# The front by single k-tiles, squares in halves, four steps ahead, one row moved from pair 3 to pair 4

## The chip, the cores and the metric

One Trainium2 chip, one of its cores. The metric is the device time of one execution in microseconds, the median of several runs. The engines are PE (TensorE matmul; PEld is its weight load), DVE (VectorE), ACT (ScalarE), POOL (GpSimd) and SP (SyncE, which only issues DMAs here).

## What is computed

Two transformer blocks on 256 tokens of width 2048, all in float32. The first block, at whose beginning the change lies, is this (cut):

```python
mod = silu(c) @ w_ada + b_ada                       # c: (1, 2048), w_ada: (2048, 6144)
shift, scale, gate = jnp.split(mod, 3, axis=-1)
h = rms_norm(x, g) * (1.0 + scale[:, None]) + shift[:, None]
proj = jnp.einsum('bsd,df->bsf', h, w_in)           # 7168 columns
q_a, k_a, v_a, z_a, q_r, k_r, v_r, z_r = jnp.split(proj, IN_SPLIT_IDX, axis=-1)
# dilated attention, retention in both directions, gates, output projection, residual
```

The second block has differential attention, a shared K/V and forgetting attention, with three more modulation vectors of the same kind and projections of 2048 rows.

## The kernel before

**Weight steps.** All weights come in steps of 128 x 1024 float32 (512 KB), two k-tiles of 128 rows times a chunk of 512 columns. SP loads a step into raw (8 slots). ACT casts it to w_hi (4 slots, L1190, split_high), a rounded float whose product with another such PE takes in one pass. DVE takes the rest, raw - w_hi, into w_lo (L1652, split_low). PE adds three products for each tile: hi by w_hi (L814), hi by w_lo (L815), lo by w_hi (L816). That makes 12 matmuls in a step. The cast of step m waits until PE has ended step m - 4.

**The front.** Steps 0 to 79 (FRONT) are the projections q, k, v and the retention's parts, ten chunks of 512 columns (numbers 0 to 9) by 16 k-tiles. They begin before the whole activation is there: for k-tile kt, h needs entries kt of shift and scale, and each of these needs one row of w_ada (transposed, 1 MB) times silu(c). So there are 32 rows (numbers 0 to 31; rows 2kt and 2kt + 1 belong to k-tile kt). POOL loads a row into gw (3 slots, L683, function load) once the row three before has been used; DVE reduces it (L1660, gemv_step), and with the second row of a k-tile makes mod and scales (L1668, L1673, head_finish). ACT then makes hi and hi + lo of the k-tile (L1519, L1523, head_kt), and DVE takes lo (L1680, head_low). Chunks are summed in two parts (PARTED tells how many k-tiles the first has): the first part leaves its PSUM bank with ACT's keep_part (L1551), the second is added by DVE's add_part (L1715).

**Who does what when.** In front() ACT and DVE each go through the steps m = 2 to 83 in order, with hand-written tables of what comes behind the split of which step: ROW_AT (row g on DVE), LOW_AT (low part of k-tile kt on DVE) and SHIFT_AT (the k-tile on ACT). Rows 32 to 47, the gate's, lie in pairs 3 and 4; a pair is 16 steps, and the steps n = 64 to 79 are pair 4, where the attention of the first block runs too. PAIR_TILES gives the rows of a pair and gemv_steps their places. Row 48 and all behind it need silu of c_2, which POOL loads when row 47 has been used.

**Queues.** SP issues x's tile 1, the vectors, then the steps: step k waits until PE has used step k - 8, and for the first 24 (LEAD_STEPS) until split k - 6 (HEAD_LEAD) is done. Step 0 is issued once tile 1 of x has landed, step 2 once row 2 has. POOL issues rows 0 and 1 when the first half of tile 0 of x has landed, computes x's inverse root (L707, L717), and issues row 2 when step 0 has landed.

**The very start.** PE spreads c over the partitions (L777), ACT takes silu of it in four pieces (L1500) and squares tile 0 of x (L1506), DVE squares tile 1 (L1687), POOL makes the root, ACT and DVE scale one tile each (L1511, L1691), PE transposes (L787), ACT keeps the eight banks (L1535, head_keep).

Of the kernel before, what the change touches and what calls it, by code (L numbers as in the profile page):

```python
# [159 lines left out]
def gemv_steps(pair):  # L160

    n = PAIR_TILES.get(pair, 0)
    first = HEAD_TILES + sum(k for p, k in PAIR_TILES.items() if p < pair)


    if pair == 4:
        return [(h, first + i) for i, h in enumerate((0, 1, 3, 4, 6, 9, 10))]
    begin, end = {3: (0, 16), 5: (0, 15), 8: (1, 9), 18: (1, 9), 22: (0, 7), 9: (6, 16), 19: (5, 16)}.get(pair, (1, 14))
    return [(begin + i * ((end - begin) / n), first + i) for i in range(n)]
# [131 lines left out]
def two_blocks(nc, a, out):  # L301
# [34 lines left out]
    with ExitStack() as ctx:  # L336
# [81 lines left out]
        bias_first = sem("bias_first")  # L418
        x_begun = sem("x_begun")
        x_landed = [sem(f"x_landed{tt}") for tt in range(TT)]  # L420
# [45 lines left out]
        c_spread = sem("c_spread")  # L466
        xhat_ready = sem("xhat_ready")
        scales_ready = sem("scales_ready")
# [150 lines left out]
        def _(sp):  # L619


            sp.dma_start(c_row, a["c"]).then_inc(c_landed[0], 16)
            for n in range(2):
                cols = slice(n * D // 2, (n + 1) * D // 2)
                sp.dma_start(resid[:, 1, cols], a["x"][0, P:2 * P, cols]).then_inc(x_landed[1], 16)
            sp.dma_start(vecs[:], a["t_vecs"]).then_inc(vecs_landed, 16)
            sp.wait_ge(x_landed[1], 32)

# [41 lines left out]
        def _(pool):  # L670
# [24 lines left out]
            def inverse_root(key):  # L695
# [8 lines left out]
                elif key[0] == "x":  # L704
                    pool.wait_ge(consts_ready, 1)
                    pool.wait_ge(x_squared, TT)
                    nc.gpsimd.tensor_scalar(mean_sq[:], square_sums[:], 1.0 / D, NORM_EPS,  # L707
                                            ALU.mult, ALU.add).then_inc(x_meaned, 1)
                    pool.wait_ge(x_meaned, 1)
# [61 lines left out]
        def _(pe):  # L771
            def head():
# [6 lines left out]
                pe.wait_ge(ident_landed, 16)  # L779
                pe.wait_ge(xhat_ready, TT)  # L780
                for r in range(TURNS):
                    if r == 4:
                        pe.wait_ge(silu_ready, 1)
                    for tt in range(TT):
# [6 lines left out]
            def front_step(n):  # L791

                if n < 2:
                    pe.wait_ge(head_kept, 4 * (n + 1))
                for q, kt in FRONT[n]:
# [381 lines left out]
        def _(act):  # L1177

            for n, landed in enumerate((x_begun, x_landed[0])):
                cols = slice(n * D // 2, (n + 1) * D // 2)  # L1180
                act.dma_start(resid[:, 0, cols], a["x"][0, 0:P, cols]).then_inc(landed, 16)
            act.dma_start(ident[:], a["t_ident"]).then_inc(ident_landed, 16)
# [313 lines left out]
            def head_x():  # L1496

                def spread_silu(n):
                    act.wait_ge(c_spread, n + 1)
                    return nc.scalar.activation(c_act[:, n * CHUNK:(n + 1) * CHUNK], banks[4 + n][:], ACT.Silu)  # L1500

                spread_silu(0)
                spread_silu(1)
                act.wait_ge(x_begun, 16)
                act.wait_ge(x_landed[0], 16)
                nc.scalar.activation(area[:, Q, 0], resid[:, 0], ACT.Square,  # L1506
                                     accum_out=square_sums[:, 0:1]).then_inc(x_squared, 1)
                spread_silu(2)
                spread_silu(3).then_inc(silu_ready, 1)
                act.wait_ge(root_ready, 1)  # L1510
                nc.scalar.activation(area[:, Q, 0], resid[:, 0], ACT.Copy, scale=rstd[:, 0:1]).then_inc(xhat_ready, 1)  # L1511

# [110 lines left out]
        def _(dve):  # L1623
# [59 lines left out]
            def head():  # L1683

                nc.vector.memset(ones, 1.0).then_inc(ones_ready, 1)
                dve.wait_ge(x_landed[1], 32)
                nc.vector.tensor_tensor_reduce(out=area[:, Q, 1], in0=resid[:, 1], in1=resid[:, 1], scale=1.0,  # L1687
                                               scalar=0.0, op0=ALU.mult, op1=ALU.add,
                                               accum_out=square_sums[:, 1:2]).then_inc(x_squared, 1)
# [680 lines left out]
```

## Time and profile before

| | us |
|---|---|
| median of 3 runs (lowest, highest) | 1442.14 (1441.98, 1442.36) |
| the profiled execution's own time | 1439.39 |
| its span, first to last instruction | 1437.6 |
| first weight matmul (L814) begins | 21.91 |
| PE busy in the span | 1405.9 (98%) |

A page of the profile gives the busy time of each engine, the span in 40 slices, and groups of instructions by line. In the timeline a line is: start in us, duration in us, engine, line of the code, operation, what is written from what, and in brackets how long the engine had been idle and what released it. A matmul's duration there (0.39 us) is longer than its turn, since matmuls overlap: the distance between starts counts.

### The profile page before, as it was taken

Reading aid. Unit: us, or ns where it says so; the run is one execution under the profiler, and the core shown is the slowest. Engines: PE = TensorE matmul, PEld = TensorE weight load, DVE = VectorE, ACT = ScalarE, POOL = GpSimd, SP = SyncE. Lnnn points to the kernel's source line nnn. Section 1 sums busy time; section 2 is a strip of 40 time slices with the busy share of each in tenths; the row PEclk is TensorE's granted clock in tenths of the full one; section 3 lists DMA queues with packets and bytes.
Section 4 is the critical chain, followed back from the end, with each engine's and each line's share of the span. In section 5 each row is a group of like instructions: output and inputs, shape, how many; then the busy total and the mean of one; then the engine's idle time right before and its main releaser. Section 6 shows DMA issues by size and latency. Waiting matters only on the chain.

```text
span 1437.6 us, 19794 instructions
## 1 busy us (share of the span) xinstructions
PE 1405.9 (98%) x6934; PEld 1175.3 (82%) x6934; DVE 1190.0 (83%) x1533; ACT 708.1 (49%) x1039; POOL 141.2 (10%) x233
## 2 busy tenths in 40 slices
PE   6999999999999999999999999999999999999996
PEld 4778888888888788888888888878888888888885
DVE  6899899888998889898878789988797877667566
ACT  5554434755435644444455553464345545465441
POOL 1111011003100001110011100010010002110000
PEclk9999999999999999999999999999999999999999
DMA  9999999888996899999977799589799688775762
GB/s 356 412 411 415 413 403 384 314 310 301 413 415 214 297 346 382 403 377 367 350 227 253 241 347 407 192 295 357 255 348 341 211 312 273 230 251 174 266 192 98
DMA packets 101624, 450.97 MB, mean 314 GB/s; under 512 B 11729, under 2 KB 16161, under 8 KB 77857
## 3 DMA queue, kind: packets, MB, share of 16 engines
q1 hardware_dynamic: 68690, 247.63, 48.2%
q0 software_dynamic: 25584, 185.63, 33.4%
q10 hardware_dynamic: 7264, 16.55, 3.1%
q8 instruction: 55, 0.90, 0.3%
q14 instruction: 31, 0.25, 0.0%
HBM read 447.62 MB, written 2.15 MB: 313 GB/s over the span
## 4 chain that ended last, share of the span: by engine, by line
PE 87%; DVE 5%; DMA 3%; issue 2%; ACT 1%; POOL 0%; DVEq 0%; SPq 0%; ACTq 0%
PE bank L879 16%; PE bank L881 16%; PE bank L880 16%; PE bank L862 15%; PE bank L860 8%; PE bank L814 3%; PE bank L816 3%; PE bank L815 3%; PE bank L1109 2%; DVE gw L1660 2%; DMA raw<-in_t_steps 2%; PE bank L1067 2%; DVE w_lo L1652 2%; PE bank L858 1%; PE bank L827 1%
## 5 line engine op out<-in xcount | busy, mean ns | idle before, releaser
L1190 ACT CAST w_hi<-raw 128x1024 fp32r<-128x1024 f32 x436 | 457.6, 1051 | 611.0 <-PE bank L881 286.8
L1635 DVE TENSOR_TENSOR w_lo<-raw,w_hi 128x1024 fp32r<-128x1024 f32 x360 | 438.5, 1225 | 176.4 <-ACT w_hi L1190 174.9
L1660 DVE CUSTOM_DVE_ANT_0 gw<-gw,c_act 128x2048 f32<-128x2048 f32 x176 | 402.3, 2287 | 0.2 <-DMA gw<-in_t_mod 0.2
L880 PE MATMUL bank<-w_lo,act_parts 128*128 128x512 f32 x1024 | 398.8, 389 | 0.0
L879 PE MATMUL bank<-w_hi,act_parts 128*128 128x512 f32 x960 | 386.5, 403 | 0.6 <-issue 0.5
L881 PE MATMUL bank<-w_hi,act_parts 128*128 128x512 f32 x960 | 375.0, 391 | 0.0
L862 PE MATMUL bank<-act_parts,w_hi 128*128 128x512 f32 x960 | 338.4, 395 | 0.0
L860 PE MATMUL bank<-act_parts,w_lo 128*128 128x256 f32 x1024 | 276.9, 281 | 0.0
L880 PEld LDWEIGHTS bank<-w_lo,act_parts 128*128 128x128 f32 x1024 | 192.6, 188 | 38.0
L862 PEld LDWEIGHTS bank<-act_parts,w_hi 128*128 128x128 f32 x960 | 180.1, 188 | 39.2
L881 PEld LDWEIGHTS bank<-w_hi,act_parts 128*128 128x128 f32 x960 | 180.2, 188 | 38.9
L879 PEld LDWEIGHTS bank<-w_hi,act_parts 128*128 128x128 f32 x960 | 180.4, 188 | 37.7 <-issue 2.4
L860 PEld LDWEIGHTS bank<-act_parts,w_lo 128*128 128x128 f32 x1024 | 192.9, 188 | 5.5
L814 PE MATMUL bank<-w_hi,act_parts 128*128 128x512 f32 x320 | 127.6, 399 | 9.9 <-DVE act_parts L1680 6.1
L816 PE MATMUL bank<-w_hi,act_parts 128*128 128x512 f32 x320 | 125.2, 391 | 0.0
L815 PE MATMUL bank<-w_lo,act_parts 128*128 128x512 f32 x320 | 125.1, 391 | 0.0
L1652 DVE TENSOR_TENSOR w_lo<-raw,w_hi 128x1024 fp32r<-128x1024 f32 x84 | 101.2, 1222 | 11.9 <-ACT w_hi L1190 11.9
L683 POOL DMA_DIRECT2D gw<-in_t_mod x96 | 52.2, 544 | 548.5 <-DVE products L1660 534.3
L814 PEld LDWEIGHTS bank<-w_hi,act_parts 128*128 128x128 f32 x320 | 60.4, 189 | 26.3 <-issue 8.0
L816 PEld LDWEIGHTS bank<-w_hi,act_parts 128*128 128x128 f32 x320 | 60.4, 189 | 12.9
L815 PEld LDWEIGHTS bank<-w_lo,act_parts 128*128 128x128 f32 x320 | 60.5, 189 | 12.1
L683 POOL DMA_DIRECT2D gw<-in_t_ada x48 | 25.6, 533 | 198.4 <-DVE products L1660 190.5
(197 smaller groups left out, 1073.7 us busy)
## 6 DMA issues: line engine op xcount, KB each, us to landing
raw<-in_t_steps SPq DMA_DIRECT2D x464, 512.0 KB, 6.5
gw<-in_t_mod POOLq DMA_DIRECT2D x96, 1024.0 KB, 8.2
gw<-in_t_ada POOLq DMA_DIRECT2D x48, 1024.0 KB, 8.4
gw<-in_t_kv_mod POOLq DMA_DIRECT2D x32, 1024.0 KB, 8.2
area<-gate_rows ACTq DMA_DIRECT2D x3, 1024.0 KB, 13.3
bias<-forget_sums ACTq DMA_DIRECT2D x16, 192.0 KB, 6.4
area<-in_ln_g ACTq DMA_DIRECT2D x2, 1024.0 KB, 8.1
area<-in_ln_b ACTq DMA_DIRECT2D x2, 1024.0 KB, 12.2
```

The source lines that it names most:

```text
L814: nc.tensor.matmul(dst, hi, w_hi[:, n % LEAD, i], start=(kt == first), stop=False)
L815: nc.tensor.matmul(dst, hi, w_lo[:, n % SLOTS, i], start=False, stop=False)
L816: last = nc.tensor.matmul(dst, lo, w_hi[:, n % LEAD, i], start=False, stop=(kt == stop - 1))
L860: last = nc.tensor.matmul(bank[:, 0:SEQ], lo[:, cols], act_hi[:, kt], start=False, stop=False)
L862: last = nc.tensor.matmul(bank[:], hi[:, cols], act_parts[:, kt].rearrange("p b t -> p (b t)"), start=False, stop=(kt == KT - 1))
L879: nc.tensor.matmul(dst, hi, w[:, k], start=(kt == 0), stop=False)
L880: nc.tensor.matmul(dst, hi, w_lo[:, j % SLOTS, k], start=False, stop=False)
L881: return nc.tensor.matmul(dst, lo, w[:, k], start=False, stop=(kt == KT - 1))
L1190: nc.scalar.copy(w_hi[:, b], raw[:, j % SLOTS]).then_inc(hi_ready, 1)
L1635: nc.vector.tensor_tensor(w_lo[:, j % SLOTS], raw[:, j % SLOTS], w_hi[:, j % LEAD].bitcast(F32), ALU.subtract).then_inc(lo_ready, 1)
L1652: nc.vector.tensor_tensor(w_lo[:, j % SLOTS], raw[:, j % SLOTS], w_hi[:, j % LEAD].bitcast(F32), ALU.subtract).then_inc(lo_ready, 1)
L1660: nc.vector.tensor_tensor_reduce(out=w, in0=w, in1=c_act[:].rearrange("p (t n) -> p t n", t=TT), scale=1.0, scalar=0.0, op0=ALU.mult, op1= ...
```

## The change

Six things, all at the beginning. (1) FRONT's steps mostly hold one k-tile of two chunks and no longer two k-tiles of one chunk, where k-tiles are new; the same products are summed in the same banks. (2) x is squared in halves on both engines, into two columns that POOL adds; ACT scales tile 0 in halves, and the transposes start with the first. (3) HEAD_LEAD is 4, not 6; SP's step 0 waits for row 0 and no longer for x; POOL's rows 0 and 1 wait for the second piece of the spread c, row 2 for row 1, and row 4 for row 3 as well. (4) ROW_AT, LOW_AT and SHIFT_AT have new places. (5) ACT keeps two banks, casts step 0, keeps one, makes k-tile 0 and casts step 1, then keeps the rest; PE waits for as many kept banks as it overwrites; DVE waits for the vectors behind rows 0 and 1; add_part stands ahead of the split. (6) Pair 3 has 8 rows and not 9, pair 4 has 8 and not 7, with the last at half step 12.

```diff
-PAIR_TILES = {3: 9, 4: 7, 5: 10, ...
+PAIR_TILES = {3: 8, 4: 8, 5: 10, ...
-FRONT = [((0, 0), (1, 0)), ((2, 0), (4, 0)), ((2, 1), (4, 1)), ((0, 1), (1, 1))]
-FRONT += [((q, kt), (q, kt + 1)) for q, kt in
-          [(3, 0), (5, 0), (8, 0), (6, 0), (8, 2), (6, 2), (0, 2), (1, 2), (9, 0), (9, 2), (9, 4), (6, 4), (0, 4),
-           (1, 4), (7, 0), (7, 2), (7, 4), (0, 6), (1, 6), (6, 6), (7, 6)]
-          + [(q, kt) for q in (2, 4, 3, 5) for kt in (2, 4, 6)]
-          + [(q, kt) for kt in (8, 10, 12, 14) for q in (2, 4, 3, 5)]
-          + [(q, kt) for q in (0, 1, 8, 9, 6, 7) for kt in range(PARTED[q], KT, 2)]]
+FRONT = [((0, 0), (1, 0)), ((2, 0), (4, 0)), ((2, 1), (4, 1)), ((0, 1), (1, 1)), ((3, 0), (3, 1)), ((5, 0), (5, 1)),
+         ((8, 0), (8, 1)), ((6, 0), (6, 1))]
+FRONT += [((p, kt), (q, kt)) for kt in (2, 3) for p, q in ((8, 6), (0, 1))]
+FRONT += [((9, kt), (9, kt + 1)) for kt in (0, 2)]
+FRONT += [((p, kt), (q, kt)) for kt in (4, 5) for p, q in ((9, 6), (0, 1))]
+FRONT += [((7, kt), (7, kt + 1)) for kt in (0, 2, 4)]
+FRONT += [((p, kt), (q, kt)) for kt in (6, 7) for p, q in ((0, 1), (6, 7))]
+FRONT += [((q, kt), (q, kt + 1)) for q in (2, 4, 3, 5) for kt in (2, 4, 6)]
+FRONT += [((p, kt), (q, kt)) for kt in range(8, KT - 2) for p, q in ((2, 4), (3, 5))]
...
-HEAD_LEAD, LEAD_STEPS = 6, 24
-ROW_AT = {4: 4, 5: 5, 6: 6, 7: 7, 8: 9, 9: 10, 10: 12, 11: 13, 12: 15, 13: 16, 14: 18, 15: 20}
-ROW_AT.update({g: 22 + int((g - 16) * 1.65) for g in range(16, HEAD_TILES)})
-LOW_AT = {1: 2, 2: 6, 3: 8, 4: 12, 5: 14, 6: 18, 7: 21}
+HEAD_LEAD, LEAD_STEPS = 4, 24
+ROW_AT = {4: 4, 5: 5, 6: 6, 7: 8, 8: 10, 9: 12, 10: 14, 11: 15, 12: 17, 13: 19, 14: 21, 15: 22}
+ROW_AT.update({g: 24 + int((g - 16) * 1.65) for g in range(16, HEAD_TILES)})
+LOW_AT = {1: 2, 2: 6, 3: 9, 4: 13, 5: 16, 6: 21, 7: 23}
-SHIFT_AT = {1: 3}
-SHIFT_AT.update({kt: ROW_AT[2 * kt + 1] + (3 if kt < 8 else 2) for kt in range(2, KT)})
+SHIFT_AT = {1: 2, 2: 6, 3: 10, 4: 14, 5: 18, 6: 22, 7: 25}
+SHIFT_AT.update({kt: ROW_AT[2 * kt + 1] + 2 for kt in range(8, KT)})
...
-            sp.wait_ge(x_landed[1], 32)
...
+                if k == 0:
+                    sp.wait_ge(gw_landed[0], 16)
...
-                    pool.wait_ge(x_squared, TT)
-                    nc.gpsimd.tensor_scalar(mean_sq[:], square_sums[:], 1.0 / D, NORM_EPS,
+                    pool.wait_ge(x_squared, 2 * TT)
+                    nc.gpsimd.tensor_tensor(mean_sq[:], most_squares[:], square_sums[:], ALU.add
+                                            ).then_inc(x_meaned, 1)
+                    pool.wait_ge(x_meaned, 1)
+                    nc.gpsimd.tensor_scalar(mean_sq[:], mean_sq[:], 1.0 / D, NORM_EPS,
...
-            pool.wait_ge(x_begun, 16)
+            pool.wait_ge(c_spread, 2)
             load(0)
             load(1)
             inverse_root(("x",))
-            pool.wait_ge(raw_landed[0], 16)
+            pool.wait_ge(gw_landed[1], 16)
             for g in range(2, HEAD_TILES + GEMV_RING):
+                if g == 4:
+                    pool.wait_ge(gw_landed[0], 32)
                 load(g)
...
-            head_step(0)
-            for r in range(6):
+            for r in range(2):
+                head_keep(r)
+            head_step(0)
+            head_keep(2)
+            head_kt(0)
+            head_step(1)
+            for r in range(3, TURNS):
                 head_keep(r)
...
+                    if n >= 0:
+                        add_part(n)
                     split_low(m)
```

## Rows read from the trace of the kernel before

**Rows 1.** The page: busy us and share of the span of each engine.

```profile
PE 1405.9 (98%) x6934; PEld 1175.3 (82%) x6934; DVE 1190.0 (83%) x1533; ACT 708.1 (49%) x1039; POOL 141.2 (10%) x233
```

**Rows 2.** Windows: stretch, length, busy of PE, PEld, DVE, ACT, POOL; clock; DMA share; GB/s.

```profile
16.50:18.50 2.00, 2.00 (x13) 2.00 (x12) 2.00 (x3) 2.00 (x4) 1.13 (x2) 1.00 0.34 63
28.00:90.00 62.00, 54.93 (x230) 43.82 (x231) 55.35 (x68) 35.80 (x49) 6.86 (x13) 0.97 1.02 411
90.00:155.00 65.00, 64.85 (x285) 53.07 (x284) 64.52 (x74) 35.31 (x46) 7.39 (x14) 1.00 1.02 416
175.00:215.00 40.00, 39.32 (x175) 31.94 (x174) 40.00 (x43) 15.50 (x15) 4.22 (x8) 1.00 1.02 403
```

**Rows 3.** Timeline, 8 to 22 us, all engines.

```profile
9.65 2.29 DVE L1687 CUSTOM_DVE_ANT_0 area<-resid 128x2048 f32<-128x2048 f32 x1 [8.67 <-DMA resid<-in_x]
12.41 0.72 POOL L717 TENSOR_TENSOR rstd<-mean_sq,minus_half 128x2 f32<-128x2 f32 x1
14.37 2.28 DVE L1660 CUSTOM_DVE_ANT_0 gw<-gw,c_act 128x2048 f32<-128x2048 f32 x1
15.31 5.01 PE L787 MATMUL bank<-ident,area 128*128 128x128 f32 x32 [5.51 <-ACT area L1511]
16.29 1.05 ACT L1190 CAST w_hi<-raw 128x1024 fp32r<-128x1024 f32 x1 [1.12 <-DMA raw<-in_t_steps]
```

**Rows 4.** Timeline and windows (columns as in rows 2), 21 to 34 us.

```profile
21.91 0.47 PE L814 MATMUL bank<-w_hi,act_parts 128*128 128x512 f32 x1 [1.59 <-DVE act_parts L1680]
23.18 1.23 DVE L1652 TENSOR_TENSOR w_lo<-raw,w_hi 128x1024 fp32r<-128x1024 f32 x1 [1.42 <-ACT w_hi L1190]
28.10 1.04 ACT L1190 CAST w_hi<-raw 128x1024 fp32r<-128x1024 f32 x1 [4.95 <-DMA raw<-in_t_steps]
32.10 0.77 PE L814 MATMUL bank<-w_hi,act_parts 128*128 128x512 f32 x1 [4.49 <-DVE act_parts L1680]
...
28.00:30.00 2.00, 0.00 (x0) 0.00 (x0) 1.93 (x5) 1.66 (x2) 0.53 (x1) 1.00 1.01 412
32.00:34.00 2.00, 1.90 (x5) 1.54 (x6) 2.00 (x2) 1.19 (x2) 0.00 (x0) 0.50 1.02 422
```

**Rows 5.** Timeline, 45 to 85 us: k-tile 2, step 8, the cast of step 22.

```profile
45.10 0.43 DVE L1680 TENSOR_TENSOR act_parts<-side,act_parts 128x256 fp32r<-128x256 f32 x1 [3.79 <-ACT side L1523]
52.66 0.50 PE L814 MATMUL bank<-w_hi,act_parts 128*128 128x512 f32 x1 [0.67 <-DVE w_lo L1652]
84.53 1.05 ACT L1190 CAST w_hi<-raw 128x1024 fp32r<-128x1024 f32 x1 [1.67 <-PE bank L816]
```

**Rows 6.** DMA queues (q0 rows, q1 steps): 31 to 38, then 28 to 90 us.

```profile
q0 software_dynamic: 258, 1.97, 67.3%
q1 hardware_dynamic: 263, 0.95, 33.9%
raw<-in_t_steps SPq DMA_DIRECT2D x2, 512.0 KB, 12.3
...
q1 hardware_dynamic: 3250, 11.83, 47.3%
raw<-in_t_steps SPq DMA_DIRECT2D x21, 512.0 KB, 7.8
```

**Rows 7.** The same view, 18.5 to 25.5 us.

```profile
q1 hardware_dynamic: 12, 0.05, 1.8%
```

**Rows 8.** Chain that ended last, near 156 us, and the timeline near 200 us.

```profile
155.94 12.43 DMA raw<-in_t_steps
...
200.32 0.47 PE L814 MATMUL bank<-w_hi,act_parts 128*128 128x512 f32 x1 [0.68 <-DVE w_lo L1652]
```

**Rows 9.** Timeline of POOL and ACT, 249 to 263 us; landing of c_act.

```profile
249.85 0.53 POOL L680 DMA_DIRECT2D c_act<-in_c  x1 [3.08 <-DVE products L1660]
262.52 1.28 ACT L1494 ACT_TABLE_LOAD   x1
...
DMA to landing us min/median/max: 6.3/6.3/6.3
```

More of the change, by code:

```diff
@@ L114 @@
               {2: 0, 4: 1, 3: 3, 5: 2, 0: 0, 1: 1, 8: 0, 9: 1, 6: 0, 7: 1})
-FRONT = [((0, 0), (1, 0)), ((2, 0), (4, 0)), ((2, 1), (4, 1)), ((0, 1), (1, 1))]
-FRONT += [((q, kt), (q, kt + 1)) for q, kt in
-          [(3, 0), (5, 0), (8, 0), (6, 0), (8, 2), (6, 2), (0, 2), (1, 2), (9, 0), (9, 2), (9, 4), (6, 4), (0, 4),
-           (1, 4), (7, 0), (7, 2), (7, 4), (0, 6), (1, 6), (6, 6), (7, 6)]
-          + [(q, kt) for q in (2, 4, 3, 5) for kt in (2, 4, 6)]
-          + [(q, kt) for kt in (8, 10, 12, 14) for q in (2, 4, 3, 5)]
-          + [(q, kt) for q in (0, 1, 8, 9, 6, 7) for kt in range(PARTED[q], KT, 2)]]
+FRONT = [((0, 0), (1, 0)), ((2, 0), (4, 0)), ((2, 1), (4, 1)), ((0, 1), (1, 1)), ((3, 0), (3, 1)), ((5, 0), (5, 1)),
[7 more added lines that the diff above has]
+FRONT += [((p, kt), (q, kt)) for kt in range(8, KT - 2) for p, q in ((2, 4), (3, 5))]
+FRONT += [((2, 14), (4, 14)), ((2, 15), (3, 14)), ((4, 15), (5, 14)), ((3, 15), (5, 15))]
+FRONT += [((q, kt), (q, kt + 1)) for q in (0, 1, 8, 9, 6, 7) for kt in range(PARTED[q], KT, 2)]
 FRONT_STEPS = len(FRONT)
-HEAD_LEAD, LEAD_STEPS = 6, 24
-ROW_AT = {4: 4, 5: 5, 6: 6, 7: 7, 8: 9, 9: 10, 10: 12, 11: 13, 12: 15, 13: 16, 14: 18, 15: 20}
-ROW_AT.update({g: 22 + int((g - 16) * 1.65) for g in range(16, HEAD_TILES)})
-LOW_AT = {1: 2, 2: 6, 3: 8, 4: 12, 5: 14, 6: 18, 7: 21}
+HEAD_LEAD, LEAD_STEPS = 4, 24
+ROW_AT = {4: 4, 5: 5, 6: 6, 7: 8, 8: 10, 9: 12, 10: 14, 11: 15, 12: 17, 13: 19, 14: 21, 15: 22}
+ROW_AT.update({g: 24 + int((g - 16) * 1.65) for g in range(16, HEAD_TILES)})
+LOW_AT = {1: 2, 2: 6, 3: 9, 4: 13, 5: 16, 6: 21, 7: 23}
 LOW_AT.update({kt: ROW_AT[2 * kt + 1] + 2 for kt in range(8, KT)})
-SHIFT_AT = {1: 3}
-SHIFT_AT.update({kt: ROW_AT[2 * kt + 1] + (3 if kt < 8 else 2) for kt in range(2, KT)})
+SHIFT_AT = {1: 2, 2: 6, 3: 10, 4: 14, 5: 18, 6: 22, 7: 25}
+SHIFT_AT.update({kt: ROW_AT[2 * kt + 1] + 2 for kt in range(8, KT)})
 BY_TOKEN, BY_UNIT = range(2)
@@ L166, in gemv_steps @@
     if pair == 4:
-        return [(h, first + i) for i, h in enumerate((0, 1, 3, 4, 6, 9, 10))]
+        return [(h, first + i) for i, h in enumerate((0, 1, 3, 4, 6, 9, 10, 12))]
     begin, end = {3: (0, 16), 5: (0, 15), 8: (1, 9), 18: (1, 9), 22: (0, 7), 9: (6, 16), 19: (5, 16)}.get(pair, (1, 14))
@@ L418, in two_blocks @@
         bias_first = sem("bias_first")
-        x_begun = sem("x_begun")
+        x_begun = [sem(f"x_begun{tt}") for tt in range(TT)]
         x_landed = [sem(f"x_landed{tt}") for tt in range(TT)]
@@ L466, in two_blocks @@
         c_spread = sem("c_spread")
-        xhat_ready = sem("xhat_ready")
+        xhat_ready = [sem(f"xhat_ready{tt}") for tt in range(TT)]
         scales_ready = sem("scales_ready")
@@ L509, in two_blocks @@
         diagonal = bias[:, 1, CHUNK - P:CHUNK]
+        x_half = [slice(n * D // 2, (n + 1) * D // 2) for n in range(2)]
+        half_sums = (most_squares, square_sums)
         c_row, ones = area[0:1, V, 0], side[0:1, 0, 0:P]
@@ L622, in _ @@
             sp.dma_start(c_row, a["c"]).then_inc(c_landed[0], 16)
-            for n in range(2):
-                cols = slice(n * D // 2, (n + 1) * D // 2)
-                sp.dma_start(resid[:, 1, cols], a["x"][0, P:2 * P, cols]).then_inc(x_landed[1], 16)
+            for n, landed in enumerate((x_begun[1], x_landed[1])):
+                sp.dma_start(resid[:, 1, x_half[n]], a["x"][0, P:2 * P, x_half[n]]).then_inc(landed, 16)
             sp.dma_start(vecs[:], a["t_vecs"]).then_inc(vecs_landed, 16)
-            sp.wait_ge(x_landed[1], 32)
             def decay_load(n):
@@ L779, in head @@
                 pe.wait_ge(ident_landed, 16)
-                pe.wait_ge(xhat_ready, TT)
+                pe.wait_ge(xhat_ready[1], 1)
+                pe.wait_ge(xhat_ready[0], 1)
                 for r in range(TURNS):
                     if r == 4:
+                        pe.wait_ge(xhat_ready[0], 2)
                         pe.wait_ge(silu_ready, 1)
@@ L809, in front_step @@
                     first, stop = (PARTED[q], KT) if later else (0, PARTED[q])
+                    if n < 2:
+                        pe.wait_ge(head_kept, 2 * (bank_of(q, 0) + 1))
                     for tt in range(TT):
@@ L1177, in _ @@
         def _(act):
-            for n, landed in enumerate((x_begun, x_landed[0])):
-                cols = slice(n * D // 2, (n + 1) * D // 2)
-                act.dma_start(resid[:, 0, cols], a["x"][0, 0:P, cols]).then_inc(landed, 16)
+            for n, landed in enumerate((x_begun[0], x_landed[0])):
+                act.dma_start(resid[:, 0, x_half[n]], a["x"][0, 0:P, x_half[n]]).then_inc(landed, 16)
             act.dma_start(ident[:], a["t_ident"]).then_inc(ident_landed, 16)
@@ L1500, in spread_silu, with square_half @@
                     return nc.scalar.activation(c_act[:, n * CHUNK:(n + 1) * CHUNK], banks[4 + n][:], ACT.Silu)
+                def square_half(n):
+                    nc.scalar.activation(area[:, Q, 0, x_half[n]], resid[:, 0, x_half[n]], ACT.Square,
+                                         accum_out=half_sums[n][:, 0:1]).then_inc(x_squared, 1)
                 spread_silu(0)
+                act.wait_ge(x_begun[0], 16)
+                square_half(0)
                 spread_silu(1)
-                act.wait_ge(x_begun, 16)
+                spread_silu(2)
                 act.wait_ge(x_landed[0], 16)
-                nc.scalar.activation(area[:, Q, 0], resid[:, 0], ACT.Square,
-                                     accum_out=square_sums[:, 0:1]).then_inc(x_squared, 1)
-                spread_silu(2)
+                square_half(1)
                 spread_silu(3).then_inc(silu_ready, 1)
                 act.wait_ge(root_ready, 1)
-                nc.scalar.activation(area[:, Q, 0], resid[:, 0], ACT.Copy, scale=rstd[:, 0:1]).then_inc(xhat_ready, 1)
+                for x in x_half:
+                    nc.scalar.activation(area[:, Q, 0, x], resid[:, 0, x], ACT.Copy, scale=rstd[:, 0:1]
+                                         ).then_inc(xhat_ready[0], 1)
             def head_kt(kt):
@@ L1685, in head @@
                 nc.vector.memset(ones, 1.0).then_inc(ones_ready, 1)
[L1686 to L1689, printed above, removed]
+                for n, landed in enumerate((x_begun[1], x_landed[1])):
+                    dve.wait_ge(landed, 16)
+                    x = resid[:, 1, x_half[n]]
+                    nc.vector.tensor_tensor_reduce(out=area[:, Q, 1, x_half[n]], in0=x, in1=x, scale=1.0, scalar=0.0,
+                                                   op0=ALU.mult, op1=ALU.add, accum_out=half_sums[n][:, 1:2]
+                                                   ).then_inc(x_squared, 1)
                 dve.wait_ge(root_ready, 1)
                 nc.vector.tensor_scalar(area[:, Q, 1], resid[:, 1], rstd[:, 1:2], None, ALU.mult
-                                        ).then_inc(xhat_ready, 1)
-                dve.wait_ge(vecs_landed, 16)
+                                        ).then_inc(xhat_ready[1], 1)
                 gemv_step(0)
                 gemv_step(1)
+                dve.wait_ge(vecs_landed, 16)
                 head_finish(0)
```

12 lines of the change are left out of this document (2 added, 10 removed).

## The prediction

> **What bounds the kernel now.** I read the page first: PE is busy 98% of the span, so only places where PE stands still are worth anything [rows 1]. The change touches the front alone (the first 80 weight steps, until about 264 us), so I cut that stretch up by time [rows 2]: PE loses most of its time before 28 us and between 28 and 90 us (54.93 busy of 62), next to nothing later. The same rows show that from 28 us on the transfers run at 411 to 416 GB/s with a share of 1.02, and that DVE is busy 64.52 of 65 us from 90 to 155. Three things are nearly full at once there. The timeline then shows the start [rows 3], the stall before step 2 [rows 4] and the two stalls after it [rows 5]; the queues' shares and the times to landing are in [rows 6, 7].
>
> A front step is 12 matmuls at a pitch of 0.227 us (0.68 us from one L814 to the next, 21.91 apart, [rows 4]), so 2.72 us.
>
> **The start, part by part.** Now both halves of token tile 1 land at 9.65, its squares take 2.29 us of DVE, POOL's root ends at 13.13, DVE's scaling at 14.37 [rows 3]. With halves, only the second half's squares follow the landing: about 1.15 + 0.08 for the sum. That gives 10.9 instead of 11.95. POOL gets one more tiny operation; the trace has none like it, so I bound it by nothing and by the 0.72 us of the root beside it [rows 3], and take 0.27, the distance between the two operations that POOL has there now. Root at 12.35 (gain 0.8). ACT's half squares (two of about 1.0 us) end before DVE's. The scaling ends at 13.6, row 0 is reduced to 15.8 and row 1 to 18.1 at 2.21 us each, the first scales are there at 18.5 (now 19.27). ACT's copy in halves lets the transposes start at 13.7 instead of 15.31.
>
> SP now asks for step 0 only when row 0 has landed, about 12.1 instead of 9.65. Two rows already fill the queue until about 15, so step 0 lands about 17.2 instead of 16.27. ACT then casts it (1.05 [rows 3]), keeps one bank and makes k-tile 0 (0.5 and 1.1, the distances between the same lines in the timeline; from 18.75); DVE's low part takes 0.43 [rows 5]. PE begins at about 20.5 instead of 21.91: **1.4 us**. Cast 1 comes right behind k-tile 0 (20.9) and no longer behind two keeps; DVE loses its wait of 1.42 us [rows 4]. I take nothing for the finer head_kept waits, since each keep (0.5 us) is done before its bank is asked for.
>
> **Step 2.** Row 4 waits for row 3, and SP sends four steps ahead. Step 2 now lands at 28.10, ACT having waited 4.95 us for it [rows 4]; in the 7 us of [rows 7] the steps get 0.05 MB, while rows 3 and 4 go through. With row 4 held back, step 2 should land by 25 or 26. Then DVE is late next: w_lo 1 until 22.15, rows 2 and 3 until 26.65, scales 27.0, w_lo 2 and k-tile 1 (which ACT now makes at step 2, not behind cast 3) until 28.7. Step 2 starts at 28.75 instead of 32.10: 3.35 us in all, 1.4 of them from the start. PE's idle stretch shrinks from 4.9 to 2.85 us. In the present kernel the granted clock is 0.50 from 32 to 34 us, the lower of its two levels, 1.2 instead of 2.4 GHz [rows 4]: matmuls start 0.43 us apart instead of 0.227, for about 8 of them, worth 1.6 us. The bound is 0 to 1.6; I take all of it, since the clock is still 1.00 in the slice from 28 to 30 us [rows 4], when the new pause is over.
>
> **Steps 3 to 19.** From there I step through the three engines with the durations of [rows 3, 4, 5]: a row 2.21 plus 0.35 for the scales of each second one, a split 1.14, a k-tile 1.1 on ACT and 0.4 on DVE, cast m not before step m-4 has ended. Now DVE waits 3.79 us at 45.10 for k-tile 2, which ACT makes two steps later than DVE asks for it [rows 5]; SHIFT_AT 2 moves from 8 to 6, and that wait goes. What is late next: ACT stands at step 6 for row 5's scales (37.45) with two casts and the keep of chunk 3 behind it, and PE's step 6 waits for that keep: 1.1 us, at about 40. Step 8, which needs k-tile 2, begins at 46.2 instead of 52.66 [rows 5]. One k-tile at a time gives the odd k-tiles two more steps, so rows 8 to 15 fit. Three k-tiles (3, 5 and 7) are still asked for by DVE one or two steps before ACT makes them, and ACT's turn there hangs on PE; each leaves PE under 0.4 us late. Step 19 begins at 75.9, against 84.53 now [rows 5]: the engines alone would gain **8.6 us**.
>
> **What the transfers take back.** The bytes to be had by a given time don't grow with the gain. The new start fills the hole of 16.5 to 18.5 us (63 instead of 413 GB/s [rows 2]: 0.7 MB) and loses some 0.25 MB around step 0, so 0.45 MB are won. Steps take 0.193 MB/us (0.524 in 2.72 us). Rows come one in 1.65 steps, 0.233 MB/us, and come two steps (5.4 us) later than before by step count. With a gain g, steps can thus land earlier by (0.45 - 0.233 (g - 5.4)) / 0.193. The tightest place now is step 52: SP sends it at 155.94, when step 44 has ended, and it lands at 168.37 [rows 8]. PE asks for it 7 steps later, 175.0. Cast, split and hand-over take 2.4, so 4.2 us are to spare. g = 4.2 + 2.3 - 1.21 g + 6.5 gives **g = 5.9**. Its bounds: 4.9 if no byte is won at the start, and 8.6 if the rows' later turn lets the steps pass. I take 5.9.
>
> **Pair 3 and 4.** DVE is busy 40.00 of 40 us from 175 to 215 [rows 2], and PE waits 0.68 us for a split there [rows 8]. One row less in that stretch (2.21 us of DVE) takes that and the smaller waits beside it: 0.7. add_part moved ahead of the split costs DVE nothing, but delays one split by 1.2 to 2.4 us at each of nine steps; the row taken away covers it, without it this would cost up to 0.5. In pair 4 the row returns at half step 12, and row 47 ends 7 us later. Behind it wait POOL's load of c_2 (issued at 249.85, 6.3 us to landing) and ACT's silu at 262.52 [rows 9]: landing at 263.3 would hold ACT 0.8 us, and the split behind it has some 4 us to spare. Zero.
>
> **Sum.** 5.9 + 0.7 = 6.6 us off the profiled execution's 1439.39, so 1432.8. The median of the runs is 2.75 higher, 1442.14, and I take the same off it: **1435.5 us**. After the front nothing changes and PE is nearly always busy, so what is won stays.
>
> **A rule against four ahead.** In [rows 6] the two queues move almost the same number of packets (258 and 263), but 1.97 against 0.95 MB, rows in packets twice as long. The Trainium skill (DMA: Bandwidth & Descriptors, Queues, rings and completion order) says that a DMA engine takes a whole packet from each queue in turn; the trace agrees. By that rule a step takes 3.8 us (0.524 MB at 139 GB/s) as long as a row is in flight, longer than PE's 2.72. Over 28 to 90 us the steps got 11.83 MB all the same, one per 2.75 us [rows 6], because rows pause.
>
> **Rivals.** (1) Transfers keep up: the rows' extra gap lets steps in and nothing is given back; 8.6 + 0.7 off, 1432.8. Against it stands the share of 1.02. Chance 0.15. (2) The new waits on landings leave the DMA queues empty as between 16.5 and 18.5 us, once or twice more (2 us each): the 0.45 MB turn into -0.8, g is 3.0, with pair 3 about 3.7 off, 1438.4. Chance 0.16. (3) The same with more holes, or the saved stalls return at step 52 altogether: under 2.9 off, about 1440. Chance 0.10. (4) **Slower:** four ahead is too short. A step is sent when the split four before it is done, so four steps take landing + cast + split, 2.3 us over the landing. In 28 to 90 us the median landing is 7.8 us [rows 6], 10.1 in all, under PE's 10.9. But around 31 to 38 us it was 12.3. Four steps then take more than PE's 10.9 from 8.6 us on, and from about 10.0 us on the 18 steps until 24 lose more than the 6.6 us won; at 11.0 us they lose 18 x 0.61 = 11.0, so 4.4 more than is won: 1446.5. Against it: the long landings had eight steps queued. Chance 0.05.
>
> **How the numbers follow.** The forecast (5 to 8 off, 1434.1 to 1437.1) has 0.54. The range 1432.7 to 1439.8 takes in rivals 1 and 2 and some of 3. A difference of 0.2% (2.9 us) is about what a measurement of this kernel tells from none. Faster by more: 0.54 + 0.15 + 0.16 = 0.85; same 0.10; slower 0.05.
>
> **What would show it.** Right: first L814 near 20.5, second stall ending near 28.8 with the clock at 1.00 after it, no wait of DVE near 45, a PE wait for ACT's keep near 40, ACT waiting for steps near 150 to 165. Wrong: PE waiting for w_lo between 45 and 90 with ACT waiting for steps (rival 4), stretches under 300 GB/s after 20 us (rival 2).

## The result

| | us |
|---|---|
| before, median of 8 runs (lowest, highest) | 1441.67 (1440.51, 1443.40) |
| after, median of 8 runs (lowest, highest) | 1445.28 (1443.51, 1447.48) |
| ratio, 95% interval | 1.0025 (1.0017 to 1.0034) |
| profiled execution, before and after | 1439.39 and 1443.51 |

The kernel became slower by 3.6 us. Forecast were 6.6 us less. This is the side of the fourth rival (steps four ahead are too few), not of the forecast.

The start came as forecast. These lines of the timeline and of the windows are of the kernel after; PE's lines were L814 and L1085 before and are L832 and L1103 now, ACT's cast is L1207, DVE's k-tile L1704:

```profile
20.23 0.47 PE L832 MATMUL bank<-w_hi,act_parts 128*128 128x512 f32 x1 [1.58 <-DVE act_parts L1704]
28.26 0.47 PE L832 MATMUL bank<-w_hi,act_parts 128*128 128x512 f32 x1 [2.34 <-DVE act_parts L1704]
...
28.00:32.00 4.00, 3.74 (x17) 3.12 (x18) 2.85 (x4) 2.29 (x3) 0.00 (x0) 1.00 1.02 425
```

The first line answers to 21.91 in [rows 4], the second to 32.10. The granted clock stays at 1.00 (2.4 GHz) behind the second, where it had stood at 0.50 (1.2 GHz) before. That is so in this trace; a later trace of the same kernel differs there (experiment 15). So at step 2 the kernel after is 3.8 us ahead. It loses that and more within 70 us:

```profile
42.82 0.50 PE L832 MATMUL bank<-w_hi,act_parts 128*128 128x512 f32 x1 [3.42 <-ACT area L1575]
53.96 0.43 DVE L1704 TENSOR_TENSOR act_parts<-side,act_parts 128x256 fp32r<-128x256 f32 x1 [3.58 <-ACT side L1546]
75.09 0.42 DVE L1704 TENSOR_TENSOR act_parts<-side,act_parts 128x256 fp32r<-128x256 f32 x1 [2.61 <-ACT side L1546]
75.67 0.47 PE L832 MATMUL bank<-w_hi,act_parts 128*128 128x512 f32 x1 [2.83 <-DVE act_parts L1704]
90.09 0.43 DVE L1704 TENSOR_TENSOR act_parts<-side,act_parts 128x256 fp32r<-128x256 f32 x1 [4.08 <-ACT side L1546]
...
60.00:90.00 30.00, 26.72 (x117) 21.47 (x115) 23.09 (x28) 13.67 (x18) 2.64 (x5) 1.00 0.97 374
...
175.00:215.00 40.00, 40.00 (x178) 33.14 (x177) 39.27 (x41) 15.82 (x15) 3.96 (x8) 1.00 1.02 413
```

PE stands before step 6 (42.82) for ACT's keep, and three times DVE stands for a k-tile (3, 5 and 6) that ACT hasn't made. PE gets over the first of the three, and stands 2.83 us at 75.67 behind the second, 1.12 us at 90.67 behind the third, and 1.32 us at 98.26. In 60 to 90 us PE is busy for 26.72 of 30 us and the transfers fall to 374 GB/s, where the rows of before show 411 over 28 to 90 us [rows 2]. From 175 to 215 us, on the other hand, PE now never stands (39.32 of 40 in [rows 2]).

The chain of waits that ended last, from 62 to 78 us, tells why DVE stands. The columns are start, duration and what was waited for:

```profile
64.18 1.23 DVE w_lo L1676
...
65.43 7.50 DMA raw<-in_t_steps
...
72.95 0.02 ACT w_hi L1207
...
73.91 0.60 ACT act_parts L1542
74.50 0.50 ACT side L1546
```

DVE's split of step 14 ends at 65.41. Only then may SP send step 18 (HEAD_LEAD 4), which takes 7.50 us to land. ACT makes k-tile 5 behind the cast of step 18 (SHIFT_AT 18), but DVE asks for it behind the split of step 16 (LOW_AT 16) and splits and reduces nothing until it has it. So a transfer that begins two splits earlier has to end before DVE may go on. This is a closed loop over DVE, SP, the DMA queue and ACT, and PE isn't in it. The chain shows the same for k-tile 3 and step 10 (10.90 us from 40.89) and for k-tile 6 and step 22 (7.90 us from 80.03). The waits of 20 to 105 us, in all, times and the longest, show it as ACT's wait for steps, while its casts hardly ever wait for PE; first after, then before:

```profile
ACT w_hi L1207 <- DMA raw<-in_t_steps: 28.8, 17, 5.4
DVE act_parts L1704 <- ACT side L1546: 10.3, 3, 4.1
...
ACT w_hi L1207 <- PE bank L834: 0.3, 1, 0.3
```

```profile
ACT w_hi L1190 <- DMA raw<-in_t_steps: 9.3, 5, 4.9
DVE act_parts L1680 <- ACT side L1523: 6.9, 4, 3.8
```

A marker behind the front shows what is left at its end, the first line before, the second after:

```profile
268.71 0.66 PE L1085 MATMUL bank<-ident,probs 128*128 128x128 f32 x4 [0.56 <-ACT qk_t L1408]
```

```profile
270.42 0.66 PE L1103 MATMUL bank<-ident,probs 128*128 128x128 f32 x4 [0.65 <-ACT qk_t L1425]
```

1.7 us of the 4.1 between the two profiled executions are there at that place. The largest piece of the rest lies in 400 to 600 us, where the windows show PE busy for 197.95 of 200 us, against 199.41 before; PE stands 1.12 us at 416.26, in code that the change doesn't touch. The lead-6 kernel of experiment 1 has that stall too (1.12 us at 410.33), so it isn't what makes the two differ. It is not explained. PE's busy time in 400 to 600 us is 197.95 to 198.01 us in the traces of the kernel after, of experiment 1 and of experiment 15, and 199.1 to 199.2 in those of experiments 2 and 13. So up to 1.2 us of a difference between two traces can lie there, and the marker tells more of the front than the time of a profiled execution does.

### The profile page after: what moved, and what is told of

It reads as the page before. It is cut to its first block, busy times and chain, and to the rows that moved or that the text cites. A ratio compares the mean times of both kernels' runs of the same rounds, so it can differ in the third digit from the quotient of the medians.

```text
span 1441.4 us, 19816 instructions
## 1 busy us (share of the span) xinstructions
PE 1406.5 (98%) x6934; PEld 1175.3 (82%) x6934; DVE 1190.3 (83%) x1535; ACT 709.4 (49%) x1042; POOL 143.0 (10%) x234
## 4 chain that ended last, share of the span: by engine, by line
PE 86%; DVE 5%; DMA 5%; issue 2%; ACT 1%; POOL 0%; DVEq 0%; SPq 0%; ACTq 0%; POOLq 0%
PE bank L880 15%; PE bank L897 15%; PE bank L899 15%; PE bank L898 15%; PE bank L878 8%; PE bank L832 3%; PE bank L834 3%; PE bank L833 3%; DMA raw<-in_t_steps 3%; DVE gw L1684 3%; PE bank L1127 2%; PE bank L1085 2%; DVE w_lo L1676 1%; PE bank L876 1%; PE bank L845 1%
## 5 line engine op out<-in xcount | busy, mean ns | idle before, releaser
L1207 ACT CAST w_hi<-raw 128x1024 fp32r<-128x1024 f32 x436 | 457.3, 1051 | 617.2 <-PE bank L899 290.4
L832 PE MATMUL bank<-w_hi,act_parts 128*128 128x512 f32 x320 | 127.3, 398 | 13.2 <-DVE act_parts L1704 9.2
L832 PEld LDWEIGHTS bank<-w_hi,act_parts 128*128 128x128 f32 x320 | 60.5, 189 | 29.2 <-DVE w_lo L1676 8.5
```

Source lines behind the costliest of these rows:

```text
L832: nc.tensor.matmul(dst, hi, w_hi[:, n % LEAD, i], start=(kt == first), stop=False)
L1207: nc.scalar.copy(w_hi[:, b], raw[:, j % SLOTS]).then_inc(hi_ready, 1)
```

## The experiments

Four theories. **A**: the closed loop above; it needs both the short lead and the late places in SHIFT_AT. **B**: the transfers alone bound the front, as the forecast's equation had it. **C**: row 4's wait for row 3, and k-tile 2 ahead of the keep. **D**: the short lead costs by itself. All ratios are to the kernel before on the same chip; each kernel ran 5 to 12 times.

**1. HEAD_LEAD 6 in the kernel after.**

```diff
-HEAD_LEAD, LEAD_STEPS = 4, 24
+HEAD_LEAD, LEAD_STEPS = 6, 24
```

> The changed kernel with HEAD_LEAD back at 6. Theory A, a closed loop: DVE asks for k-tiles 3, 5 and 7 one or two steps before ACT makes them, ACT's casts there wait for a step's data, and SP sends that step only when DVE's split four earlier is done. The loop needs both the short lead and the late place. By A the waits of DVE for ACT's k-tile (10.3 us between 20 and 105 us) shrink to under 3 us and PE's stalls at 75.67, 90.67 and 98.26 (5.3 us) go: 5 us under the changed kernel, ratio to before 0.998 to 1.000. Theory B, the transfers alone bound the front (all that PE wins is given back whatever the lead): within 1 us of the changed kernel, ratio 1.002 to 1.003. Theory C, row 4's wait for row 3 and the k-tile 2 placed ahead of the keep (stall of 3.4 us at 42.82) are the cost: at most 1 to 2 us better.

Measured: 1435.89 us, ratio 0.9962 (0.9949 to 0.9976). One number gives back 9 us, more than A expected (0.998 to 1.000). In its profile:

```profile
DVE act_parts L1704 <- ACT side L1546: 4.0, 5, 1.3
...
43.76 0.55 PE L832 MATMUL bank<-w_hi,act_parts 128*128 128x512 f32 x1 [4.22 <-ACT area L1575]
...
60.00:90.00 30.00, 29.91 (x132) 24.51 (x131) 27.65 (x36) 16.08 (x21) 3.29 (x7) 1.00 1.01 412
...
81.45 1.06 ACT L1207 CAST w_hi<-raw 128x1024 fp32r<-128x1024 f32 x1 [1.67 <-PE bank L834]
```

DVE's waits for k-tiles fall from 10.3 to 4.0 us, none over 1.3 (A had said under 3 in all), the transfers are back at 412 GB/s, and the marker is at 264.41, 6.0 us ahead of the kernel after and 4.3 ahead of the kernel before. The last line is the cast of step 22, which PE's step 19 follows: 3.1 us ahead of the same cast in [rows 5]. B falls. The stall before step 6 stays. A and D both allow this result.

**2. K-tiles 3 to 7 on ACT where DVE asks for them, lead 4.**

```diff
-SHIFT_AT = {1: 2, 2: 6, 3: 10, 4: 14, 5: 18, 6: 22, 7: 25}
+SHIFT_AT = {1: 2, 2: 6, 3: 9, 4: 13, 5: 16, 6: 21, 7: 23}
```

> The changed kernel with ACT making k-tiles 3 to 7 at the very steps where DVE asks for them (SHIFT_AT = LOW_AT: 9, 13, 16, 21, 23), lead 4 kept. Theory A: the loop is opened at its other end, the same 5 us come back, ratio 0.998 to 1.000; DVE's waits for ACT's k-tile under 2 us. Theory D, the short lead costs by itself (a step's landing plus cast and split is longer than four steps of PE): ACT still waits over 20 us for steps and at most 1 to 2 us come back, ratio 1.0015 to 1.003. Theory B: no change.

Measured: 1439.72 us, 0.9988 (0.9979 to 0.9997). 5 us come back, as A said, and DVE never waits for a k-tile. But ACT still waits 22.4 us for steps, which D had expected, the transfers stay at 376 GB/s in 60 to 90 us, and the marker (268.14) is only 2.3 us ahead of the kernel after. A new stall stands in its timeline; with both edits (3.) it is 4.51 us, at 63.25:

```profile
62.73 0.50 PE L832 MATMUL bank<-w_hi,act_parts 128*128 128x512 f32 x1 [2.82 <-ACT area L1575]
```

K-tile 4, moved from step 14 to 13, waits for row 9's scales on ACT, and the keep of chunk 8, which step 12 needs, stands behind it.

**3. Both edits.**

> Both edits at once: HEAD_LEAD 6 and SHIFT_AT = LOW_AT. Theory A: opening the loop twice brings no more than opening it once, within 1.5 us of the better of the two. Theory D: clearly better than the place alone (by 2 us or more). Theory B: all three as the changed kernel. If what is left over is theory C, all three keep a PE stall of about 3 us near 42 us.

Measured: 1437.68 us, 0.9976 (0.9966 to 0.9987), 0.0014 worse than the lead alone; the intervals overlap. Its median is 1.8 us above the better of the two, where A allowed 1.5, and 2.0 us (1.7 by the ratios) under the place alone, where D asked for 2 or more: by these bounds it decides nothing. What does tell is the comparison: with the places aligned, the lead is worth 0.0012; with the late places it was worth 0.0063. The two act together, which is A. The alignment has a price in both kernels, the stall before step 12, here 4.5 us with the granted clock at 0.50 from 62 to 68 us behind it; so 2 and 3 don't measure the loop alone.

**4. HEAD_LEAD 4 in the kernel before.**

```diff
-HEAD_LEAD, LEAD_STEPS = 6, 24
+HEAD_LEAD, LEAD_STEPS = 4, 24
```

> The kernel before with HEAD_LEAD 4 and nothing else. Its tables too let DVE ask for k-tiles 2, 3, 5, 6 and 7 one or two steps before ACT makes them. Theory A: the loop closes here too, DVE's waits for ACT's k-tile rise from 6.9 to over 10 us and the kernel loses 3 to 8 us, ratio 1.002 to 1.006. Theory D: the same sign. Theory B: within 1 us of the kernel before. So this tells B from the other two, and e2 tells A from D.

Measured: 1446.45 us, 1.0037 (1.0023 to 1.0050). The short lead alone makes the kernel before slower by 5 us. (In its tables k-tile 4 is late by one step too, 13 against 12.) This excludes B and, as said beforehand, can't tell A from D. The waits of its trace, 20 to 105 us (6.9 us in the kernel before):

```profile
DVE act_parts L1680 <- ACT side L1523: 14.0, 5, 4.9
```

**5. Row 4 without its wait for row 3, lead 6.**

```diff
-                if g == 4:
-                    pool.wait_ge(gw_landed[0], 32)
```

> Changed kernel with HEAD_LEAD 6 (1435.89 by itself, ratio 0.9962) and, here, row 4 no longer waiting for row 3. There PE still stands 4.2 us before step 6 (43.76): ACT waits 4.5 us for row 5's scales and the keep of chunk 3 stands behind; DVE waited 1.7 us for row 5 to land. Theory C1, the gate makes rows 4 and 5 late: without it that stall falls to 1 to 2 us, 2 to 3 us better, ratio about 0.994. Theory C2, the gate pays for itself: step 2 lands 2 to 3 us later again (28 instead of 25 us) and the gain is lost, ratio 0.996 to 0.998.

Measured: 1436.19 us, 0.9966 (0.9955 to 0.9978), no difference to 0.9962. Both C1 and C2 are right in their part: the stall before step 6 is gone altogether, and step 2 begins at 29.74 instead of 28.38, with an idle stretch of 3.69 instead of 2.34 us. The gate trades one stall for another: without it the granted clock is 0.50 from 30 to 34 us, behind the longer stall before step 2, and with it 0.52 and 0.63 from 44 to 48 us, behind the stall before step 6.

**6. K-tile 2 later, lead 6.**

```diff
-LOW_AT = {1: 2, 2: 6, 3: 9, ...
+LOW_AT = {1: 2, 2: 7, 3: 9, ...
-SHIFT_AT = {1: 2, 2: 6, 3: 10, ...
+SHIFT_AT = {1: 2, 2: 8, 3: 10, ...
```

> Changed kernel with HEAD_LEAD 6, and k-tile 2 made on ACT at step 8 (not 6), its low part on DVE behind step 7 (not 6), so that the keeps and casts of steps 6 to 8 no longer stand behind row 5's scales. If the order on ACT makes the stall before step 6 (4.2 us), it falls under 1.5 us and 2 to 3 us come back, ratio about 0.994. If k-tile 2 then comes late for step 8, a stall of the same size moves there and the ratio stays at 0.996.

Measured: 1437.93 us, 0.9976 (0.9964 to 0.9989), no better than the 0.9962 without it. The stall before step 6 falls to 1.09 us as expected, others of 0.65 and 1.66 us come at 60 and 73 us. So the order on ACT did make that stall, and its removal bought nothing that can be measured.

**7. The rows of pairs 3 and 4 as before, lead 6.**

```diff
-PAIR_TILES = {3: 8, 4: 8, ...
+PAIR_TILES = {3: 9, 4: 7, ...
-        return [(h, first + i) for i, h in enumerate((0, 1, 3, 4, 6, 9, 10, 12))]
+        return [(h, first + i) for i, h in enumerate((0, 1, 3, 4, 6, 9, 10))]
```

> Changed kernel with HEAD_LEAD 6 and the rows of pairs 3 and 4 as before (9 and 7). The forecast had 0.7 us for the moved row. By it this is 0.5 to 1 us slower than with the row moved, ratio 0.9966 to 0.9970, and PE waits for splits again between 190 and 215 us. If the row's move is worth nothing, 0.996.

Measured: 1438.24 us, 0.9976 (0.9966 to 0.9986), 0.0014 or 2 us worse than with the row moved, with overlapping intervals. Its timeline has two stalls, 1.8 us together. They lie ahead of the 190 to 215 us of the expectation, and the longer one is for an add_part; the second is 0.70 us for a split, at 187.67:

```profile
178.47 0.51 PE L832 MATMUL bank<-w_hi,act_parts 128*128 128x512 f32 x1 [1.08 <-DVE area L1741]
```

This execution also began step 2 only at 31.19, which the edit can't have caused; part of the 2 us may be such scatter. Nor do the two stalls belong to the row alone: kernel 3, which has the row moved, shows them too (0.78 us at 178.05 and 0.50 at 187.25), and the traces of after and of 1 show none there. So the worth of the moved row stays open.

**8. The start and the moved row only.** FRONT, HEAD_LEAD (6) and the three tables as before.

> The changed kernel with everything between FRONT and SHIFT_AT as before (order of the steps, HEAD_LEAD 6, the three tables): what is left of the change is the start (halves of x, who waits for what, keeps, add_part's place) and the row moved to pair 4. Forecast: the start alone brings 1.4 us at the first step and 1.9 more at step 2, the stalls at 45 to 52 us stay: 3 to 4 us under before, ratio 0.9972 to 0.998. If the order by single k-tiles brings nothing, it equals the lead-6 kernel at 0.996.

Measured: 1440.15 us, 0.9991 (0.9979 to 1.0004): at most 3 us, likely 1.3, and nothing is within the interval. Step 2 begins at 28.77, 3.3 us earlier, but then PE stands 1.05 us at 40.95 and 4.06 us for a split at 48.02. The kernel before has 1.63 us at 49.02 and 0.67 at 52.66 [rows 5] in their place:

```profile
48.02 0.47 PE L828 MATMUL bank<-w_hi,act_parts 128*128 128x512 f32 x1 [4.06 <-DVE w_lo L1672]
```

**9. HEAD_LEAD 8** and **10. HEAD_LEAD 5** in the kernel after, each as in 1.

> Changed kernel with HEAD_LEAD 8, which is no limit beyond raw's eight slots. Lead 4 gave 1.0025 to before, lead 6 0.9962. If the lead costs only where a step lands later than it is asked for (theory D with A), 6 is already enough and 8 gives the same within 0.1%: 0.995 to 0.997. If more steps in the queue take turns from the rows (the reason to have a limit), rows 4 and 5 land later, PE's stall before step 6 grows beyond 4.2 us and the ratio goes back to 0.998 or more.

> Changed kernel with HEAD_LEAD 5. Theories A and D: each step less in the lead takes one split and its share of rows (2.7 us) from the time a step has to land; the queue's median landing is 8 to 10 us. By that 5 lies between, nearer to 6: ratio 0.997 to 1.000, transfers at 395 to 410 GB/s in 60 to 90 us (lead 4: 374, lead 6: 412). A threshold would show as either end.

Measured: 1437.88 us, 0.9971 (0.9960 to 0.9982) with 8; 1438.22 us, 0.9975 (0.9963 to 0.9986) with 5. So leads of 4, 5, 6 and 8 give 1.0025, 0.9975, 0.9962 and 0.9971. Three of them agree within their intervals, and 4 stands alone: nearly a threshold. With 5 the transfers move 401 GB/s in 60 to 90 us. With 8 the stall before step 6 is 1.97 us and not over 4.2, so more steps in the queue did not push rows 4 and 5 back.

**11. The order and the tables only.** The kernel before with the new FRONT, ROW_AT, LOW_AT and SHIFT_AT and HEAD_LEAD 6.

> The kernel before with the new FRONT and the new three tables, HEAD_LEAD 6, nothing of the start and no row moved. The start with the moved row alone gave 0.9991, all but the lead 0.9962. If the parts add up, the order brings 0.997 to 0.998 here, the stalls at 49 and 53 us go and one before step 6 comes. If order and start need each other, it is 0.999 to 1.001.

Measured: 1439.04 us, 0.9976 (0.9967 to 0.9986), 3.1 to 3.5 us. With 8 (0.0009) that adds up to 0.0033, and all parts together with lead 6 gave 0.0038: the parts add up, as well as intervals of 0.001 either way can tell. The stalls at 49 and 53 us are gone as expected, but none came before step 6: this kernel lacks row 4's wait.

**12. HEAD_LEAD 8 and no wait of row 4**, the edits of 9 and 5.

> Changed kernel with neither limit: HEAD_LEAD 8 and row 4 not waiting for row 3. With lead 6 the gate made no difference (0.9962 with, 0.9966 without). If both limits are worth nothing, 0.995 to 0.997 again. If at least one of them is needed to let rows 2 to 5 pass ahead of the steps, step 2 starts after 30 us and the ratio is 0.998 or more.

Measured: 1436.41 us, 0.9963 (0.9950 to 0.9976). Without either limit the kernel is as fast as with the best of them. Neither limit is worth anything that these intervals show; the one at 4 costs 9 us.

**13. Only k-tiles 3, 5 and 7 forward, lead 4,** and **14. the same with lead 6.** **15.** is the kernel after, unchanged, on their chip.

```diff
-SHIFT_AT = {1: 2, 2: 6, 3: 10, 4: 14, 5: 18, 6: 22, 7: 25}
+SHIFT_AT = {1: 2, 2: 6, 3: 9, 4: 14, 5: 16, 6: 22, 7: 23}
```

> Changed kernel, lead 4, with only k-tiles 3, 5 and 7 made by ACT at the step where DVE asks for them (SHIFT_AT 9, 16, 23 instead of 10, 18, 25). Theory A (the loop is the larger part): DVE's waits for ACT's k-tile fall from 10.3 us to under 3, no new stall near 63 us, ratio 0.996 to 0.998, most of the 9 us back. Theory D (the short lead by itself): no better than 0.9988, and ACT still waits over 20 us for steps with PE standing for them.

> The same three places with HEAD_LEAD 6. Theory A: within 0.15% of the same places with lead 4, and of lead 6 with the old places (0.9962). Theory D: 0.2% or more better than with lead 4.

> The changed kernel as it is, beside the two others on their chip. Both theories: 1.0015 to 1.0035 to the kernel before, as at first (1.0025).

Measured: 13: 1439.18 us, 0.9984 (0.9975 to 0.9993); 14: 1437.31 us, 0.9967 (0.9954 to 0.9980); 15: 1443.87 us, 1.0017 (1.0009 to 1.0026). On this chip 13 is 0.0033 (4.7 us) better than 15, and lead 6 brings 0.0017 more (2.5 us; 1.9 by the medians), where it had brought 0.0063 with the late places. In the profile of 13 ACT still waits 22.7 us for steps in 20 to 105 us, but DVE only 2.9 us for a k-tile. The measured 13 lies just outside of what A expected and the step to 14 just under what D expected; 14 is also just outside of A's 0.15%, and ACT's wait stayed over 20 us as D said. I had also picked one k-tile wrongly: the trace of after shows 6 in the loop, not 7, and in 13 its wait is the one that is left:

```profile
85.62 0.43 DVE L1704 TENSOR_TENSOR act_parts<-side,act_parts 128x256 fp32r<-128x256 f32 x1 [2.87 <-ACT side L1546]
```

On this chip the loop thus makes about two thirds of what the short lead costs (0.0033 of 0.0050; by the markers 3.8 of 5.1 us, 270.19 in 15, 266.42 in 13, 265.07 in 14). How the last third divides between k-tile 6 and the lead itself wasn't tried, so D is not excluded as the smaller part.

The trace of 15 shows one thing more. It is the same kernel as after, with the same pause before step 2, but here the clock falls behind it:

```profile
28.31 0.47 PE L832 MATMUL bank<-w_hi,act_parts 128*128 128x512 f32 x1 [2.33 <-DVE act_parts L1704]
...
30.00:32.00 2.00, 2.00 (x6) 1.52 (x6) 0.97 (x1) 0.63 (x1) 0.00 (x0) 0.50 1.02 428
```

## Why the prediction was wrong

**The start: right, the clock in part by luck.** First matmul at 20.23 (20.5 forecast), step 2 at 28.26 (28.75), the clock at 1.00 behind it. The forecast took the whole 1.6 us of the clock because the slice before was at 1.00. In the trace of 15 (the same kernel) and in those of 6, 9 and 14, with pauses of 2.30 to 2.52 us there, the clock was at 0.50 to 0.52 in 30 to 32 us; in those of after, 1, 2, 3, 8 and 13, with 2.30 to 2.57 us, it stayed at 1.00. So the middle of the range from 0 to 1.6 would have been fairer.

**Step 6: the place right, the size not.** PE stood 3.42 us for the keep behind k-tile 2, against 1.1 forecast; the granted clock then fell to 0.50 in 44 to 46 us, which the sum hadn't. The mis-sized term is row 5: DVE waited 0.70 and 1.99 us for rows 4 and 5 to land, which row 4's wait for row 3 had made late, so row 5's scales were there at 39.7 and not at 37.45. Without that wait (experiments 5, 11 and 12) no stall over 0.5 us stands before step 6.

**Steps 8 to 23: the step that failed.** The prediction said of the k-tiles that DVE asks for too early that "ACT's turn there hangs on PE; each leaves PE under 0.4 us late". ACT's turn hung on the landing of a step, and that on DVE: ACT's casts waited 28.8 us for steps and 0.3 for PE, and PE stood 2.83, 1.12 and 1.32 us. Step 19 begins 36 matmuls behind the one at 75.67, at 83.94 us, where the forecast had 75.9 and the kernel before 84.53: 0.6 us won instead of 8.6. The prediction also named too few k-tiles: by its tables 3 to 7 are all asked for before ACT makes them, and the longest wait was for 6, asked for one step early. The hand-made schedule took every step as there in time. The parts were all named, but never set beside each other: a landing of 7.8 us in the median [rows 6], SP's wait for the split four before, and a k-tile two casts behind the split that asks for it. Put together: split 14 ends, 7.5 us landing, 1.0 cast, 1.1 k-tile, 0.2 hand-over, 9.8 us, in which DVE has two splits, two rows and one k-tile's scales to do, 7.0 us; hence 2.8 us of standing (2.61 measured for k-tile 5). I had spread the lead evenly (four steps of 10.9 us against landing + 2.3), so that it began to cost at a landing of 8.6 us and cost the whole gain at 10.0; with the late places it begins to cost at about 4.7 (7.0 less 2.3; an estimate from these rows).

**The fourth rival: the right limit, half of the mechanism.** It named the lead, its sign and one of its signs in the profile (ACT waiting 28.8 us for steps instead of 9.3); that PE would wait for w_lo was wrong (0.6 us, against 9.2 for act_parts). It had nothing of the k-tile that holds DVE. Its chance of 0.05 rested on the landings of 8.6 and 10.0 us. That its 1446.5 lies near the measured 1445.28 is luck: it priced landings of 11.0 us, and at the measured median of 8.8 its own formula takes back 0.9 us (18 steps x 0.05) and leaves the kernel faster.

**The transfers' share: not tested by the kernel after, and weakened by the others.** With the lead at 6 the forecast of 1435.5 stands beside a measured 1435.89 (ratio 0.9962, forecast 0.9954). But the agreement is luck: 6.6 us were 8.6 less 2.7 for the transfers plus 0.7. In the trace with lead 6 the cast of step 22, which tells where step 19 begins, is only 3.1 us ahead of before (81.45 against 84.53), not 8.6. Of the missing 5.5 us, 3.1 are the stall before step 6 (4.22 for 1.1) and some 1.7 the clock behind it (an estimate from 0.52 and 0.63 in 44 to 48 us). From there to the marker the kernel wins another 1.2 us and gives nothing back. Near step 52 ACT does wait up to 2.71 us for a step (at 167.75), but PE doesn't stand. So the 8.6 was too large with either lead, and the 2.7 for the transfers is not borne out.

**Pair 3 and 4: not settled.** PE is busy 40.00 of 40 us from 175 to 215 in the kernel after, against 39.32, which is the 0.7 us of the forecast. But a kernel with the row moved (3) loses 1.7 us there, and one without it (7) 1.8; the 2 us between 7 and 1 have overlapping intervals. The later load of c_2 showed no cost.

**The packet rule.** The Trainium skill (DMA: Bandwidth & Descriptors, Queues, rings and completion order) has a DMA engine take turns by packet between the queues that it has work for. In the kernel after the steps' queue got 1488 packets and the rows' 781 in 60 to 90 us, 46.6% and 50.6% of the engines' time. That is not against the rule, and no test of it either: a row is asked for only when DVE has used one (POOL waits 70.7 us for DVE in 20 to 105 us), and at 374 GB/s both queues seem to have run empty at times.

## What to carry to other kernels

When a limit on a queue is tightened, follow it around: who frees the next transfer, what that engine may be waiting for at the time, and whether that wait ends only with the same transfer. Two settings that cost little or nothing measurable apart (a look-ahead of four 0.0012 to 0.0017 of the time with the places mended, the late places nothing with a look-ahead of six) closed a loop together: a look-ahead of four and a result asked for one or two steps early. And a wait that an in-order engine makes for another one costs everything queued behind it, so the tables of two engines for the same item should name the same step, unless something urgent stands behind it, as the keep did here.

## What was not expected of the hardware

A prefetch limit that was too short by one step cost 0.5% (lead 4 against 5: 1.0025 and 0.9975), while 5, 6 and 8 can't be told apart. A shorter queue hardly landed its steps sooner after their issue: the median in 28 to 90 us was 8.8 us with lead 4 and 10.3 with 6. That is 1.5 us less, for steps issued two splits later, and the DMA rate fell from 412 to 374 GB/s in 60 to 90 us.

After nearly the same pause of PE (2.3 to 2.6 us before step 2) the granted clock stayed at 1.00 in six traces and fell to 0.50 or 0.52 in four; of the kernel after there are two traces, one of either kind. The length of the pause alone doesn't tell which it will be, and no run shows what does.
